# The transposed first-level inverses of a chunked delta rule: made on VectorE from compact blocks, in place of TensorE transposes

## What is computed

```python
def gated_delta_chunked(q, k, v, g, beta):
    k_beta = k * beta[..., None]
    lmat = jnp.where(strict, jnp.einsum('bhncd,bhnsd->bhncs', k_beta, k) * decay, 0.0)
    rhs = jnp.concatenate([v * beta[..., None], k_beta * jnp.exp(g)[..., None]], axis=-1)
    sol = lax.linalg.triangular_solve(eye + lmat, rhs, left_side=True, lower=True,
                                      unit_diagonal=True)
    ...
    def step(state, inp):
        v_new = val_n - jnp.einsum('bhcd,bhde->bhce', kc_n, state)
        o_n = jnp.einsum('bhcd,bhde->bhce', qd_n, state) + jnp.einsum('bhcs,bhse->bhce', a_n, v_new)
        state = state * dl_n[..., None, None] + jnp.einsum('bhcd,bhce->bhde', kd_n, v_new)
        return state, o_n
```

## Time and profile before

| | |
|---|---|
| time, median of 3 runs | 2136.16 us (2136.07 to 2136.36) |
| the profiled execution's own time | 2140.02 us |
| its span (first to last instruction) | 2138.7 us |
| TensorE busy | 2071.2 us, 97% of the span |
| VectorE busy | 1239.0 us, 58% |
| GpSimd busy | 903.1 us, 42% |
| ScalarE busy | 860.1 us, 40% |
| chunks of layer 0 / layer 1 (`delta`) | about 1355 to 1505 us / 1830 to 1981 us of the span |

### The profile page before, as it was taken

How to read it: one execution, slowest core, us unless ns; L and a number is a source line. 1 busy time by engine, 2 the same in 40 slices (tenths; PEclk the granted TensorE clock), 3 DMA queues, 4 the chain that set the end, 5 groups by cost and what they waited for, 6 DMA issues and landing times.

```text
span 2138.7 us, 26849 instructions
## 1 busy us (share of the span) xinstructions
PE 2071.2 (97%) x10832; PEld 1652.4 (77%) x10832; DVE 1239.0 (58%) x1943; ACT 860.1 (40%) x1378; POOL 903.1 (42%) x430
## 2 busy tenths in 40 slices
PE   9999999998999999999999999999999999999998
PEld 7888888775666688888888787787778787778777
DVE  6322223846676533222223788899765779898752
ACT  4222233323444543222223465344444375344532
POOL 4444444332213344444444463544434554444443
PEclk9999999999999999999999999999999999999999
DMA  4343333321102133333333222101223222100222
GB/s 160 108 138 98 99 97 93 116 69 40 31 21 60 60 99 98 93 95 99 99 99 97 81 89 70 50 30 31 69 82 96 88 80 79 50 21 30 79 89 79
DMA packets 46186, 169.09 MB, mean 79 GB/s; under 512 B 5232, under 2 KB 6000, under 8 KB 45808
## 3 DMA queue, kind: packets, MB, share of 16 engines
q1 hardware_dynamic: 45344, 165.60, 25.0%
q10 hardware_dynamic: 720, 1.79, 0.2%
HBM read 165.27 MB, written 2.10 MB: 78 GB/s over the span
## 4 chain that ended last, share of the span: by engine, by line
PE 75%; DVE 17%; ACT 5%; issue 1%; POOL 1%; DMA 0%; ACTq 0%; DVEq 0%
PE ps L388 21%; PE ps L390 21%; PE ps L389 21%; DVE cu L1882 4%; DVE blk_t L1984 2%; DVE outer L1982 1%; PE ps L662 1%; PE ps L678 1%; PE ps L647 1%; PE ps L448 1%; ACT dl L1477 1%; ACT whi L1040 1%; PE ps L987 1%; DVE dl L2091 1%; PE ps L998 1%
## 5 line engine op out<-in xcount | busy, mean ns | idle before, releaser
L2213 POOL TENSOR_TENSOR wlo<-raw,whi 128x1024 fp32r<-128x1024 f32 x300 | 750.7, 2509 | 871.4 <-ACT whi L1040 869.8
L388 PE MATMUL ps<-xh,whi 128*128 128x512 f32 x1584 | 641.4, 405 | 11.2 <-ACT gates L1218 6.2
L390 PE MATMUL ps<-xh,wlo 128*128 128x512 f32 x1584 | 620.8, 392 | 0.0
L389 PE MATMUL ps<-xl,whi 128*128 128x512 f32 x1584 | 620.2, 392 | 0.0
L1040 ACT CAST whi<-raw 128x1024 fp32r<-128x1024 f32 x300 | 312.4, 1043 | 170.0 <-DMA raw<-in_stream 169.9
L388 PEld LDWEIGHTS ps<-xh,whi 128*128 128x128 f32 x1584 | 299.4, 189 | 104.9 <-issue 32.2
L390 PEld LDWEIGHTS ps<-xh,wlo 128*128 128x128 f32 x1584 | 298.9, 189 | 64.0
L389 PEld LDWEIGHTS ps<-xl,whi 128*128 128x128 f32 x1584 | 299.6, 189 | 59.6 <-issue 2.9
L1882 DVE SCALAR_TENSOR_TENSOR cu<-up,lcols,cu 128x512 f32<-128x512 f32 x180 | 172.2, 1007 | 0.1
L2240 POOL TENSOR_TENSOR cu<-cu,prod 128x512 f32<-128x512 f32 x60 | 87.5, 1458 | 142.9 <-ACT prod L1290 141.7
L1590 DVE TENSOR_TENSOR ml<-mid,mh 128x512 fp32r<-128x512 f32 x42 | 56.9, 1358 | 152.1 <-ACT mh L1104 152.1
(11 more groups left out here) (362 smaller groups left out, 3001.1 us busy)
## 6 DMA issues: line engine op xcount, KB each, us to landing
raw<-in_stream SPq DMA_DIRECT2D x300, 512.0 KB, 3.6
w1k<-in_w SPq DMA_DIRECT2D x1, 2048.0 KB, 8.2
w1v<-in_w SPq DMA_DIRECT2D x1, 2048.0 KB, 8.0
outT<-h SPq DMA_DIRECT2D x4, 512.0 KB, 2.7
h<-in_xT SPq DMA_DIRECT2D x2, 512.0 KB, 7.8
h<-in_xT ACTq DMA_DIRECT2D x2, 512.0 KB, 7.4
mats<-in_mats ACTq DMA_DIRECT2D x1, 448.0 KB, 10.6
msk<-in_masks SPq DMA_DIRECT2D x1, 258.0 KB, 4.0
```

The source lines that it names most:

```text
L388: pe.matmul(out, wh, hi, start=first, stop=False)
L389: pe.matmul(out, wh, lo, start=False, stop=False)
L390: return pe.matmul(out, wl, hi, start=False, stop=last)
L2213: pool.tensor_tensor(m.wlo[:, slot, :], m.raw[:, slot, :], m.whi[:, slot, :].bitcast(F32), ALU.subtract).then_inc(s.wlo)
```

## The change

`turned_inverse` on VectorE makes level 1's `b.U` without TensorE. ScalarE (`diagonal`) writes beta on the diagonal of `b.U`: four activations of 128x128 for each direction, identity times beta. VectorE transposes the chunk's compact blocks in 32x32 pieces (128x128 for the four heads) into rows of `small`, multiplies by beta in place, and puts the result over `b.U` by a predicated copy with the mirrored mask. TensorE's eight transposes a chunk (L943) and VectorE's two multiplies from PSUM (L2139 in level 1) go; the multiplies of level 2 and of the last step stay. Signals: `d_u0` is new (ScalarE's diagonal is there), `mean` and `var` of another part of the layer become one signal `cu_sum` with counts 2l+1 and 2l+2, which changes no order there. TensorE's waits for `d_t` and `d_onew` move from the removed transposes to the first products.

```diff
@@ tensor_engine, delta
-            for d, at, X, b, ts, t in both:
-                if i:
-                    pe.wait_ge(s.d_onew, at - 1)
-                pe.wait_ge(s.d_t, level_event(nl, at, 1))
-                heads(lambda n, hs: pe.transpose(X[2][:, hs], b.T[:, n, :], ident)).then_inc(s.d_u)
             fill(i, "decay")
...
                     else:
+                        pe.wait_ge(s.d_t, level_event(nl, at, 1))
                         pe.wait_ge(s.d_qd, at + 1)
                         pe.wait_ge(s.d_at, at + 1)
...
                     if lv == 1:
+                        if i:
+                            pe.wait_ge(s.d_onew, at - 1)
                         half_products(X[2], b.U, b.Y).then_inc(s.d_uy)
@@ scalar_engine
+    def diagonal(l, i):
+        for d, at, X, b, t in chunk(l, i):
+            be = m.small[:, 9, t, 4 * d:4 * d + 4]
+            if i == 0:
+                act.wait_ge(s.d_t, level_event(len(LEVELS), at, 1))
+            for n in range(DN_H):
+                ins = act.activation(b.U[:, n, :], mat(m, "ident"), ACT.Copy, scale=be[:, n:n + 1])
+            ins.then_inc(s.d_u0)
@@ scalar_engine, delta
             if i:
                 decays(l, i)
+            else:
+                diagonal(l, 0)
             fill(i, "decay")
...
                 act.copy(b.vn, X[1]).then_inc(s.d_vns)
+            if i < NT - 1:
+                diagonal(l, i + 1)
             fill(i, "values")
@@ vector_engine
+    def turned_inverse(l, i):
+
+        for d, at, X, b, t in chunk(l, i):
+            at_block, wt = 16 * d + 4 * t, turned_blocks(m, d)
+            be = m.small[:, 9, t, 4 * d:4 * d + 4].unsqueeze(2).broadcast_to([P, DN_H, BASE])
+            then(dve.transpose(wt.rearrange("p h c -> p (h c)"),
+                               m.blk_w[:, at_block:at_block + 4, :].rearrange("p h c -> p (h c)")))
+            then(dve.tensor_tensor(wt, wt, be, ALU.mult))
+            mask = m.levels[:, 1 - d, 0, :].rearrange("p (q c) -> p q c", c=BASE).unsqueeze(1)
+            dve.wait_ge(s.d_u0, at + 1)
+            dve.copy_predicated(b.U.rearrange("p h (q c) -> p h q c", c=BASE),
+                                mask.broadcast_to([P, DN_H, P // BASE, BASE]),
+                                wt.unsqueeze(2).broadcast_to([P, DN_H, P // BASE, BASE])).then_inc(s.d_us)
@@ vector_engine, delta
-                for d, at, X, b, t in both:
+                for d, at, X, b, t in both if lv > 1 else ():
                     be = m.small[:, 9, t, 4 * d:4 * d + 4]
-                    dve.wait_ge(s.d_u, level_event(nl, at, lv))
-                    dve.tensor_tensor(b.U, X[2 if lv == 1 else 1], heads4(be), ALU.mult).then_inc(s.d_us)
+                    dve.wait_ge(s.d_u, level_event(nl - 1, at, lv - 1))
+                    dve.tensor_tensor(b.U, X[1], heads4(be), ALU.mult).then_inc(s.d_us)
                 if lv == 1:
                     if i:
                         decayed_keys(l, i)
+                    turned_inverse(l, i)
                     conv("decay")
```

More of the change, by code:

```diff
@@ L174 @@
     "h_new yl up wab_lo ab qconv ab_raw ab_t sq_qkv ab_read decay gl l2 cum d_kk kk_read picked d_pre d_min "
-    "filled o_sq conv shared mean cu_sq var o_dn d_snew d_vns d_onew d_t d_u d_att d_ys d_qd d_at d_y d_qk "
+    "filled o_sq conv shared cu_sum cu_sq d_u0 o_dn d_snew d_vns d_onew d_t d_u d_att d_ys d_qd d_at d_y d_qk "
     "d_us d_uy d_ttk d_ttv d_kd d_s0 d_ks d_rest d_vn d_s d_q d_o act_step raw0 raw1 raw2 raw3 in_h0 in_h1 "
@@ L263, in blocks, with turned_blocks @@
     return t[:, 16 * d:16 * d + 16, :].rearrange("p (t n) c -> p t n c", t=NT)
+def turned_blocks(m, d):
+    return m.small[:, 4 * d:4 * d + 4].rearrange("p r t n -> p r (t n)")
 def after_base(n, l, at):
@@ L864, in layer @@
         pe.wait_ge(s.shared, 30 * l + 30)
-        sum_rows(ps[:, 5, :], [m.cu[:, c, :] for c in range(4)]).then_inc(s.mean)
+        sum_rows(ps[:, 5, :], [m.cu[:, c, :] for c in range(4)]).then_inc(s.cu_sum)
         z_unit(4)
@@ L868, in layer @@
         pe.wait_ge(s.cu_sq, 4 * l + 4)
-        sum_rows(ps[:, 5, :], [m.rt[:, c, :] for c in range(4)]).then_inc(s.var)
+        sum_rows(ps[:, 5, :], [m.rt[:, c, :] for c in range(4)]).then_inc(s.cu_sum)
         z_unit(6)
@@ L1420, in layer @@
         weights_upto(u0 + L_Z + 6 + AHEAD + 1)
-        act.wait_ge(s.var, l + 1)
+        act.wait_ge(s.cu_sum, 2 * l + 2)
         then(act.activation(ps[:, 5, :], ps[:, 5, :], ACT.Ln, bias=eps, scale=1.0 / (4 * P)))
@@ L2062, in layer @@
         dve.wait_ge(s.conv, 3 * l + 3)
-        dve.wait_ge(s.mean, l + 1)
+        dve.wait_ge(s.cu_sum, 2 * l + 1)
         for c in range(4):
```

## The result

The changed kernel takes **2178.35 us**, the median of four runs from 2176.77 to 2180.86. The kernel before, in the same batch, takes 2136.11. The ratio is 1.0197, with a 95% interval of 1.0184 to 1.0210: slower by 42.2 us, where I had forecast 33.8. The time lies in the range given. The profiled run took 2180.86, with a span of 2179.6.

What follows compares the result with a forecast made beforehand. VectorE's queue up to level 1's predicated copy was taken as the bound, not busy TensorE. Per layer 2.5 + 3 x 4.8 = 16.9, two layers +33.8, on 2136.2 gave 2170.0 us; range 2142 to 2184.

Steps and rivals of the forecast that it cites:

- VectorE's queue sets the pace, and all of it counts: Second to fourth chunk: VectorE's queue sets the pace up to L2150 (now L2181), which starts 3.9 us later, all paid.
- The added multiply and copy are caught, the transpose is not: Added group: GpSimd blocks VectorE instructions with two SBUF inputs for a whole instruction; without any blocking, -1.4 us a chunk.
- The low clock: Behind L2150, second to fourth chunk: TensorE's idling brings the 1.2 GHz level; 0 to 2.4 us, taken as 0.9.
- The first chunk: Each layer's first chunk: L2150 delayed by VectorE's queue, +1.95 us and 0.5 for the clock, +2.5.
- Both go: the fill comes first, at full clock: First chunk: TensorE's 2.9 us wait for L2115 and its slow fill both disappear.
- Nothing for TensorE's removed transposes: Each later chunk: eight transposes, 0.8 us, hidden by VectorE and costed at nothing.
- nothing for ScalarE's diagonals: Chunk's end: eight added activations, 2.1 us, costed at nothing; 2.1 us a chunk if nothing covered them.
- A: The forecast itself: blocking by every GpSimd instruction, clock partly low; 2155 to 2178 us, time 2170; chance 0.58.
- D: Rival, slower by more: the low clock lasts through each chunk; +44, 2180 us; chance 0.12.
- B: Rival, slower by less: blocking stays what it was, passing from taps and scores to new instructions; +6, 2143 us; chance 0.17.
- C: Rival, faster: the new instructions aren't caught and L2150 comes earlier; -13, 2123 us; chance 0.13.
- The signs: Right: multiplies over 1 us, copies over 2, L2150 wait 3 or more, clock under 0.9; wrong: a `d_us` wait.

Runs made afterwards that it cites:

- the PSUM kernel: The changed kernel with the small transposed blocks in PSUM, so multiply and predicated copy have one SBUF input; 2159.7 us, ratio 1.0100.

## Why the prediction was right, point by point

**VectorE's queue sets the pace, and all of it counts.** Confirmed by four kernels: where the copy shifts by +0.9, +2.0, +3.3 or -2.1 us, a later chunk shifts by that much or more.

**The added multiply and copy are caught, the transpose is not.** Confirmed in kind by the PSUM kernel, in size by the trace. The forecast queue against the measured one, in us behind the mark:

| end of | forecast | measured |
|---|---|---|
| L2114 | 1.2 | 1.19 |
| first multiply | 2.7 | 2.66 |
| first copy | 5.7 | 5.49 |
| second multiply | 7.2 | 6.73 |
| second copy | 9.1 | 8.57 |
| taps | 10.4 | 9.87 |
| L2181 starts | 13.1 | 12.44 |

The forecast was 0.7 too late, so +3.9 became +3.3. Of this 0.2 stands at the first copy, where L2244 took 2.43 us, 0.3 between the copies, where the two L2271 took 3.13 us with VectorE's pieces between, and the rest in the scores.

**The low clock.** The mechanism held and its size was too small: this is the term that was most mis-sized. I took 0.9 of a bound of 2.4 us, and it is 1.1 in two chunks and 3.0 in four, over the bound, a mean of 2.4. Three things were missing. TensorE's wait for L2144 was not in the prediction: it does not delay L2181, which stands in VectorE's queue without a wait, but behind it the clock falls already ahead of the wait for L2181. I had only slowed the fill matmuls, but the transposes and products slow down too: 0.7 us for L950 and 0.44 for L929. And in a long chunk the low level lasts longer and moves the phase between the engines. In the third chunk TensorE is at 0.50 from 1455 to 1461, and VectorE's next taps meet GpSimd:

```profile
1455.00:1458.00 3.00, 1.65 (x8) 1.57 (x8) 3.00 (x5) 0.00 (x0) 0.00 (x0) 0.50 0.00 0
1458.00:1461.00 3.00, 3.00 (x22) 2.37 (x21) 1.97 (x4) 1.59 (x3) 0.00 (x0) 0.50 0.00 0
1461.00:1464.00 3.00, 3.00 (x28) 2.11 (x28) 1.23 (x2) 2.62 (x4) 0.48 (x1) 0.85 0.31 51
```

```profile
1464.03 4.11 DVE L1898 SCALAR_TENSOR_TENSOR cu<-up,lcols,cu 128x512 f32<-128x512 f32 x2
```

Those taps take 4.11 us, and L990 behind them waits up to 1.1 us for L2189 (the last row of the waits above). How the 3.0 splits between the slower matmuls and this shift was not measured apart; that both go with the clock is shown.

**The first chunk.** Forecast +2.5, measured +3.5 and +3.6. It was made up wrongly. As forecast, L2244 slipped behind ScalarE's diagonals, to 1361.12, and the second multiply took 2.12 us. But in layer 0 L2271 came only at 1364.71, so the second copy went free and L2181 started at 1369.65, 1.35 us sooner than my 1371.0 (1371.6 in the prediction is the end of its first half). TensorE began L950 0.8 us later than before, where I had 1.95. What took that gain and more lies behind, 2.6 us where I had 0.5: TensorE idled behind the fill instead of ahead of it, and then ran at half clock exactly where it was due:

```profile
1370.51 1.94 PE L950 MATMUL ps<-mats,dl 128*128 128x128 f32 x8 [2.68 <-DVE dl L2181]
...
1374.03 0.63 PE L394 MATMUL ps<-xl,whi 128*128 128x512 f32 x1
```

In layer 1 the copy was caught after all (1.70 us), L2181 came later and TensorE waited 4.10 us for it; the sum there is +3.6 by another way. The step that failed is "Both go: the fill comes first, at full clock". The fill did run at full clock, but the idle time did not go: it moved to a worse place, worth about 7 us in all by the kernel in which only that wait was put back (2171.33).

**Nothing for TensorE's removed transposes, nothing for ScalarE's diagonals.** Both confirmed by the kernels that isolate them.

**The sum.** Forecast 2 x (2.5 + 3 x 4.8) = 33.8; in the same terms measured 2 x 3.5 for the first chunks, 6 x 3.3 for the copies, 14.2 behind them: 41.0. Against the forecast the first chunks are 2.0 over, the copies 3.7 under and what lies behind them 8.8 over, so the errors partly cancel, and that is luck. The outcome lies between A and D. D's picture, the clock low through all of each chunk, is wrong, but its sum of 44 was the closer one: the low level comes in pieces and costs by what it slows. B fell on the amount: the taps' 2.3 us did pass on, but the new instructions were blocked for 4.8 us in the second chunk (multiplies 1.22 and 1.02 for 0.30 each, copies 2.79 and 1.80 for 0.74 each). C fell with the first multiply of 1.22 us.

**The signs.** Not all of those named came. The multiplies were over 1 us in the second chunk and the clock under 0.9, but only one of its two copies was over 2 us (2.79 and 1.80), and TensorE's wait for L2181 was 2.69 us there, not 3 or more. The wait for `d_us`, named as a sign of being wrong, did come (15.1 us in 9). It did not overturn the forecast, because VectorE reaches L2181 later still: the product it releases ends at 1410.39 and L2181 starts at 1413.53.

## What to carry to other kernels

Count the queue ahead of the awaited instruction on the engine that is waited for, and not the load of the busiest engine: here 64 transposes fewer on TensorE gained nothing, and matmuls that compute nothing gained 17.5 us. Where GpSimd works beside VectorE, try one input of the VectorE instruction in PSUM, as the multiply and the predicated copy had it here, or place those with two SBUF inputs where GpSimd rests; blocking that is taken off one instruction can fall on the next such one in the queue, so look behind it. Idle time on TensorE costs twice where the low clock meets work that is due. Put fill where it shortens the idle time (2137.5 to 2133.5 us in the kernel before); where it doesn't, let the wait stand ahead of the fill (2178.4 to 2171.3 in the changed one). And remove a wait whole: two edits that each shortened the queue were worth 33.4 us by their sum, and 56.5 to 59.5 together.

## What the runs showed of the hardware that I had not expected

- Small matmuls lose about the same share by the low clock as large ones (0.63 us in place of 0.39 for 512 columns): eight 128x128 transposes take 1.94 us in place of 1.24, sixteen 64x64 products 1.12 in place of 0.68.
- A predicated copy with mask and data in SBUF is caught by GpSimd like a multiply, 1.80 and 2.79 us in place of 0.74, and free with its data in PSUM though the mask stays in SBUF. A stream transpose of 128 columns takes 0.29 to 0.32 us wherever it stands.
- The drop of the clock is not in every execution. In the kernel with the diagonals alone, the first chunk of layer 0, which starts 3.0 us earlier there, ran at a granted clock of 1.00 from 1356 to 1364 behind the same two waits of 1.9 and 1.0 us, where that of before had 0.61 over a part of it; the chunk was 1.1 us shorter. Which later chunks are the short ones changes too: the second of layer 0 and the fourth of layer 1 in the changed kernel, the second and fourth of layer 0 in the one with only the wait put back.
